# Stick-breaking attention in a decoder layer: query tiles 0 and 1, and 4 and 5, share one score slot in each pair step

## What is computed

```python
def block(args):                     # one query tile of 128 rows, all heads
    qi, i = args
    tpos = i * Q_BLOCK + jnp.arange(Q_BLOCK)
    z = jnp.einsum('bhqd,bhkd->bhqk', qi, k) * SCALE
    past = kpos[None, :] < tpos[:, None]
    log_fail = jnp.where(past, jax.nn.log_sigmoid(-z), 0.0)
    after = lax.cumsum(log_fail, axis=3, reverse=True) - log_fail
    a = jnp.where(past, jnp.exp(jax.nn.log_sigmoid(z) + after), 0.0)
    return jnp.einsum('bhqk,bhkd->bhqd', a, v)
```

## Time and profile before

| | us |
|---|---|
| median of three runs (1333.78 to 1333.85) | 1333.83 |
| the profiled execution's own time | 1333.74 |
| its span, from first to last instruction | 1331.9 |
| the eight pair steps, 119.6 to 606.4 | 486.8 |

### The profile page before, as it was taken

One profiled execution on the slowest core, in us unless ns is written; L12 is line 12 of the kernel. 1 busy time (PEld: TensorE's weight loads), 2 busy tenths in 40 slices (PEclk: granted clock), 3 DMA queues, 4 the chain that ended last, 5 costly groups with the idle time before them and its releaser, 6 DMA issues.

```text
span 1331.9 us, 20551 instructions
## 1 busy us (share of the span) xinstructions
PE 1316.9 (99%) x6854; PEld 1086.6 (82%) x6854; DVE 1032.5 (78%) x1185; ACT 684.3 (51%) x1202; POOL 418.1 (31%) x307
## 2 busy tenths in 40 slices
PE   7999999999999999999999999999999999999999
PEld 5887888888888888788888788888888888888887
DVE  7578989798888889995258877878778787777866
ACT  7577666667676667773244433343343434333340
POOL 2000000000000000213035754747556484654721
PEclk9999999999999999999999999999999999999999
DMA  7100110100010101205111222121212112121103
GB/s 253 32 25 25 32 33 17 32 24 24 24 38 17 31 25 40 96 25 166 48 40 32 71 72 63 42 72 31 71 47 63 56 39 71 39 71 60 43 32 127
DMA packets 91333, 71.50 MB, mean 54 GB/s; under 512 B 4240, under 2 KB 75920, under 8 KB 91280
## 3 DMA queue, kind: packets, MB, share of 16 engines
q1 hardware_dynamic: 91280, 70.81, 17.1%
HBM read 65.03 MB, written 4.19 MB: 52 GB/s over the span
## 4 chain that ended last, share of the span: by engine, by line
PE 92%; DVE 3%; ACT 2%; POOL 1%; issue 1%; DMA 0%; SPq 0%; ACTq 0%; POOLq 0%; DVEq 0%
PE ps L1419 27%; PE ps L346 17%; PE ps L1594 14%; PE ps L1125 7%; PE ps L402 5%; PE ps L386 5%; PE ps L376 4%; PE ps L1204 3%; PE ps L312 3%; PE ps L1649 2%; PE ps L901 1%; PE ps L841 1%; ACT junk L782 1%; PE ps L1012 1%; DVE a_l L598 1%
## 5 line engine op out<-in xcount | busy, mean ns | idle before, releaser
L1604 DVE TENSOR_TENSOR x<-ps,x 128x2048 f32<-128x2048 f32 x70 | 160.3, 2289 | 92.7 <-PE ps L1594 92.6
L605 POOL TENSOR_TENSOR o_t<-o_t,pv_low 128x256 f32 x24 | 22.9, 953 | 442.7 <-ACT o_t L490 442.7
L1387 DVE TENSOR_TENSOR part_l<-part_x,part_h 128x512 fp32r<-128x512 f32 x140 | 141.7, 1036 | 25.3 <-POOL part_x L1365 17.9
L1582 POOL TENSOR_TENSOR bl<-bx_B,bh 128x512 fp32r<-128x512 f32 x70 | 93.0, 1329 | 208.9 <-ACT bh L1578 208.9
L346 PE MATMUL ps<-hh,w_h 128*128 128x512 f32 x336 | 140.6, 418 | 0.0
L478 ACT ACTIVATE a_h<-ps 128x256 fp32r<-128x256 f32 (+2 forms) x96 | 78.0, 812 | 118.6 <-PE ps L386 118.0
L346 PE MATMUL ps<-hh,w_l 128*128 128x512 f32 x336 | 132.0, 393 | 0.0
L346 PE MATMUL ps<-hl,w_h 128*128 128x512 f32 x336 | 131.3, 391 | 0.0
L1419 PE MATMUL ps<-ft_h,part_h 128*128 128x512 f32 x320 | 124.5, 389 | 0.0
L1419 PE MATMUL ps<-ft_l,part_h 128*128 128x512 f32 x320 | 124.5, 389 | 0.0
L1419 PE MATMUL ps<-ft_h,part_l 128*128 128x512 f32 x320 | 124.5, 389 | 0.0
(11 more groups left out here) (288 smaller groups left out, 3392.7 us busy)
## 6 DMA issues: line engine op xcount, KB each, us to landing
w_raw<-in_sb_w_in SPq DMA_DIRECT2D x52, 256.0 KB, 2.9
bx_B<-in_w_down SPq DMA_DIRECT2D x44, 256.0 KB, 3.0
part_x<-in_w_gate SPq DMA_DIRECT2D x40, 256.0 KB, 2.9
part_x<-in_w_up SPq DMA_DIRECT2D x40, 256.0 KB, 2.9
wo_raw<-in_w_out SPq DMA_DIRECT2D x20, 256.0 KB, 2.9
x_in<-in_x SPq DMA_DIRECT2D x8, 512.0 KB, 7.7
x<-in_x SPq DMA_DIRECT2D x16, 256.0 KB, 6.2
out<-x SPq DMA_DIRECT2D x16, 256.0 KB, 2.0
```

What stands on the lines that cost most here:

```text
L1387: dve.tensor_tensor(part_l[m][p][:, :, :].rearrange(flat), part_x[m][p][:, :, :].rearrange(flat), part_h[p][:, :, :].rearrange(flat).bitca ...
L1582: pool.tensor_tensor(bl[(par + k) % 2][:, :], bx[B_OPS[k]][:, :], bh[(par + k) % 2][:, :].bitcast(F32), ALU.subtract).then_inc(s_bw, 1)
L1604: dve.tensor_tensor(o, ps[:, 0:4], o, ALU.add).then_inc(s_x2, 1)
```

## The change

`UNITS` gets ten entries. Tiles 0 and 1 become one slot (unit 0), the late chunks of tiles 4 and 5 another (unit 3); the slot numbers in `BOTH`. In such a slot tile i-1 lies in columns 0 to 127 and tile i in columns 144 to 399, so one ACT or DVE instruction on both is 400 columns a head. The other units move up. `pe_step` is unchanged in form, so scores of two slots are made at five places of a step. The values are still summed in six groups (`GROUPS`), at the units in `VALUES_AT`. For a shared slot both tiles stand in the upper 128 columns of `a_h`, and each matmul moves 128 columns. The projection of the next pair is dealt by `PARTS`. DVE scans the first head of unit 2 at u = 0 in every step, ahead of the weights and low parts there, and at u = 1 it does `dve_weights` before `dve_low`. The tables `CONV_AT`, `LOW_AT`, `PRE_AT`, `SPLIT_RATE`, `DVE_RATE`, `FILL` and `FILLED` are dealt anew for ten units; in step 6 a seventh head half is split ahead.

```diff
+    ODD_AT = P + 16
+    SPAN = ODD_AT + 2 * P
+    UNITS = [(1, 0, SPAN, True), (2, 0, 3 * P, True), (3, 0, BANK, True), (5, BANK, SPAN, True),
+             (4, 0, BANK, False), (5, 0, BANK, False), (6, BANK, 3 * P, True), (7, BANK, BANK, True),
+             (6, 0, BANK, False), (7, 0, BANK, False)]
+    BOTH = (0, 3)
...
+    GROUPS = [(0,), (1, 2), (3,), (4, 5), (6, 7), (8, 9)]
+    VALUES_AT = {1: 0, 2: 1, 3: 2, 5: 3, 7: 4, 9: 5}
+    ROWS_AT = {2: 0, 3: 2, 6: 5}
+    PARTS = {1: (0, 5, 8), 2: (1, 0, 8), 3: (2, 0, 8), 4: (3, 0, 4), 5: (3, 4, 8), 6: (4, 0, 4), 7: (4, 4, 8),
+             8: (5, 0, 4), 9: (5, 4, 8)}
+    EVAC_LOW = {2: 0, 3: 1, 4: 2, 6: 3}
-    LOW_AT = {0: 1, 2: 2, 3: 3, 6: 4, 7: 5, 10: 6}
+    LOW_AT = {0: 1, 1: 2, 3: 3, 4: 4, 5: 5, 8: 6}
+    def tiles_of(u):
+        i, _, w, _ = UNITS[u]
+        return ((i - 1, 0, P), (i, ODD_AT, 2 * P)) if u in BOTH else ((i, 0, w),)
 def pe_values
+            if u in BOTH:
+                parts = [(0, P, 0, 1, P), (P, 2 * P, 0, 2, P), (P, 2 * P, 1, 3, P)]
+            else:
+                w_first = UNITS[u - 1][2]
+                parts = [(0 if j * P < w_first else P, 2 * P, j, j, None) for j in range(w // P)]
             for h in range(2):
+                for b, (q0, q1, j, slot, col) in enumerate(parts):
                     for t, a in enumerate((a_h, a_l)):
+                        mm = pe.matmul(o_ps[:, h * 2 * P + q0:h * 2 * P + q1],
                                        v_s[par][:, k0 // P + j, 2 * h:2 * h + 2, :].rearrange("p a d -> p (a d)"),
+                                       a[:, h, slot, q0 if col is None else col:2 * P],
 def pe_step
                     pe_part(pe, s + 1, 1 - par, 0, 0, 2)
                     pe_transposes(pe, s, u)
-                    pe_part(pe, s + 1, 1 - par, 0, 2, 4)
+                    pe_part(pe, s + 1, 1 - par, 0, 2, 5)
                 elif not last:
-                    pe_part(pe, s + 1, 1 - par, u // 2, 4 * (u % 2), 4 * (u % 2) + 4)
+                    pe_part(pe, s + 1, 1 - par, *PARTS[u])
 def dve_scan
+                for _, at_, w in reversed(tiles_of(u)):
+                    back = f[:, at_:at_ + w + 1][:, ::-1]
+                    dve.tensor_tensor_scan(back, back, own[:, BANK - w:BANK + 1][:, ::-1], 0.0, ALU.mult, ALU.max
 def dve_step
-                if last and u == 0:
+                if u == 0:
                     dve_scan(dve, s, 2, 0)
-                if nxt and u and not (last and u == 1):
+                if nxt and u > 1:
                     dve_scan(dve, *nxt, 0)
...
+                if u == 1:
+                    dve_weights(dve, *nxt)
                 dve_low(dve, s, u)
-                if nxt and u:
+                if nxt and u > 1:
                     dve_weights(dve, *nxt)
...
+        PRE_AT = {2: EX[0:3], 3: EX[3:6], 5: EX[6:], 8: [("w", 0, 0), ("w", 1, 0)], 9: [("w", 2, 0), ("w", 3, 0)],
+        FILL = {0: [(0, (2, 3, 4, 5))], 1: [(1, (0, 1, 2, 3))], 2: [(1, (4, 5))], 3: [(2, None)], 4: [(3, LOWER)],
+                5: [(3, UPPER)], 6: [(4, None)], 7: [(5, None)], 8: [(6, None)], 9: [(7, None)]}
```

More of the change, by code:

```diff
@@ L50, in trunk, with blocks_of, group_of, home_of @@
     W0 = MW + 2
-    CONV_AT = {0: (2,), 2: (3,), 4: (4,), 5: (5,), 9: (6,), 11: (7,)}
-    LOW_AT = {0: 1, 2: 2, 3: 3, 6: 4, 7: 5, 10: 6}
+    CONV_AT = {0: (2,), 2: (3,), 3: (4,), 4: (5,), 7: (6,), 9: (7,)}
+    LOW_AT = {0: 1, 1: 2, 3: 3, 4: 4, 5: 5, 8: 6}
     GR = 4
-    assert NU % 2 == 0 and NU == 12
+    assert NU == 10
+    def tiles_of(u):
+        i, _, w, _ = UNITS[u]
+        return ((i - 1, 0, P), (i, ODD_AT, 2 * P)) if u in BOTH else ((i, 0, w),)
+    def blocks_of(u):
+        return [at_ + j * P for _, at_, w in tiles_of(u) for j in range(w // P)]
+    def group_of(u):
+        return [n for n, g in enumerate(GROUPS) if u in g][0]
+    def home_of(u):
+        n = len(blocks_of(u))
+        odd = u in BOTH or u == GROUPS[group_of(u)][1]
+        return slice(1 if u in BOTH else 0, n + (1 if u in BOTH else 0)), slice(P if odd else 0, 2 * P if odd else P)
     with ExitStack() as ctx:
@@ L168, in trunk @@
         x2 = [at(f"x2_{half}", [P, NT // 2, D], F32, a) for half, a in enumerate((ex_at, al_at))]
-        EX = [("o", k, 0) for k in range(6)]
+        EX = [("o", k, 0) for k in range(6)] + [("o", 0, 1)]
         ex_h = {i: at(f"ex_h{n}", [P, BANK], F32R, ex_at + n * 2 * KB) for n, i in enumerate(EX)}
@@ L341, in pe_part @@
                     pe.wait_ge(s_el, 4 * s + p)
-            if half == 0 and lo % 4 == 0:
-                pe.wait_ge(s_wl, W0 + 6 * s + 2 * b + lo // 4 + 1)
             for kc in range(lo, hi):
+                if half == 0 and kc % 4 == 0:
+                    pe.wait_ge(s_wl, W0 + 6 * s + 2 * b + kc // 4 + 1)
                 for i, (w, h) in enumerate(((wh, hh), (wh, hl), (wl, hh))):
@@ L372, in pe_scores @@
                 pe.wait_ge(s_fg, 2 * (NU * s + u - 2) + 2)
[L373 to L377, removed]
+            for i, at_, w in tiles_of(u):
+                for t, (q, kk) in enumerate(((q_h, k_h), (q_h, k_l), (q_l, k_h))):
+                    for h in range(2):
+                        r = slice(HD * h, HD * h + HD)
+                        mm = pe.matmul(z2[u % 2][:, h, at_:at_ + w], q[par][r, i * P:(i + 1) * P],
+                                       kk[par][r, k0:k0 + w], start=(t == 0), stop=(t == 2))
             mm.then_inc(s_z, 1)
         def pe_transposes(pe, s, u):
-            _, _, w, _ = UNITS[u]
             pe.wait_ge(s_a, NU * s + u + 1)
@@ L594, in dve_low @@
         def dve_low(dve, s, u):
[L595 to L596 removed]
+            js, cols = home_of(u)
             dve.wait_ge(s_th, 1 + TUSE * s + u + 1)
[L598 to L599 removed]
+            dve.tensor_tensor(a_l[:, :, js, cols],
+                              t_ps[:, :, 0:len(blocks_of(u)) * P].rearrange("p h (j q) -> p h j q", q=P),
+                              a_h[:, :, js, cols].bitcast(F32), ALU.subtract).then_inc(s_tl, 1)
         def pool_heads(pool, s, u):
@@ L624, in dve_step @@
                 nxt = (s, u + 1) if u + 1 < NU else (s + 1, 0) if not last else None
-                if last and u == 0:
+                if u == 0:
                     dve_scan(dve, s, 2, 0)
-                if nxt and u and not (last and u == 1):
+                if nxt and u > 1:
                     dve_scan(dve, *nxt, 0)
-                if u % 2 == 0 and 0 < u < 10 and not last:
-                    dve_evac_half(dve, s + 1, u // 2 - 1, 1 - par)
+                if u in EVAC_LOW and not last:
+                    dve_evac_half(dve, s + 1, EVAC_LOW[u], 1 - par)
                 if nxt and u:
```

103 lines of the change are left out of this document (45 added, 58 removed).

## The result

The changed kernel takes **1342.02 us** (1341.69 to 1342.06, 6 runs) against 1333.85 us before: a ratio of 1.0061, 95% interval 1.0048 to 1.0074. The forecast was 1342.0.

A forecast was written before the change was run, and what follows sets the result against it. TensorE was taken to bound the kernel, busy 1316.9 of 1331.9 us. Terms 7.0 - 3.2 + 3.75 + 2.0 - 1.3 = +8.25 us on 1333.74 gave 1342.0 us, own range 1339 to 1345, wider range 1336.5 to 1346.5.

The forecast's parts named there:

- Values, +7.0: Shared slots' values on PE: twelve 128-column matmuls paced by loads 0.11 us apart, 0.44 more a group, +7.0 us.
- rival 1: Shared values: short matmuls cheaper, 0.17 us a pair or 81 ns each, term 2.2, time 1337.2 us; chance 0.13.
- rival 4: Whole kernel faster: cheap shared values, first wait covered, later waits gone, -4.8 us, 1329 us; chance 0.07.
- Score place, -3.2: Five score places instead of six a step on PE, 0.40 us saved each, -3.2 us over eight steps.
- Wait at the beginning, +3.75: Steady step's beginning: PE waits for `w_l` and `a_l` behind DVE's scan, 0.75 us a step, +3.75 us for five.
- Rival 2: Step's beginning: the wait does not appear, ScalarE reaching `fail` earlier or PE's transposes slipping anyway; 1336 us; chance 0.07.
- Steady step: Steady pair steps in the loop: 61.4 us forecast instead of 60.2.
- Step 0, +2.0 of waits: First step: longer DVE chain up to `a_l` makes PE wait 3 us, about 1 already there; net +2.0 us.
- Steps 6 and 7, -1.3 of waits: Last two steps: waits of 1.25 us each instead of 1.9, -0.65 us each.
- Other slots, 0: Slots after unit 2: VectorE stays ahead of PE, tightest dates 0.25 us early at units 5 and 9; 0 us.
- rival 3: More waits: one 0.25 us reserve lost in each step, +0.5 us a step, 1346 us; chance 0.10.

The follow-up runs named there:

- Experiment 3: Kernel after with the shared slot's three value blocks stored side by side, eight value matmuls a group instead of twelve: 1335.50 us.
- experiment 6: Kernel before with the matmuls of both 256-column value groups cut into two of 128 columns: 1347.29 us.
- experiment 7: Kernel before with only one value group (tiles 0 and 1) cut into 128-column matmuls: 1342.70 us.
- Experiment 5: Kernel after with a sixth score place in every step but the last, between two halves of a projection: 1345.06 us.
- experiment 2: Kernel after with ScalarE's `fail` of unit 2 directly behind the copy of v, ahead of the four row copies: 1337.85 us.
- experiment 1: Kernel after with VectorE making `w_l` ahead of the scan of the 512-key tile at unit 0: 1338.55 us.
- Experiment 11: Kernel after with value blocks side by side, `fail` ahead of the low rows, and VectorE's low v ahead of two splits before the last step: 1330.19 us.
- experiment 4: Kernel after with value blocks side by side, plus `w_l` ahead of the scan: 1332.02 us; or plus `fail` ahead of the low rows: 1331.38 us.
- experiment 8: Kernel before with the tiles 0 and 1 value group cut, and 64 load-and-matmul pairs more at TensorE's program start: 1344.27 us.
- experiment 9: Kernel after with one more diagonal-unit value pair cut, 16 instructions more in TensorE's loop (1655 against 1639): 1350.80 us.
- experiment 10: Kernel after with value blocks side by side, `fail` ahead of low rows, `w_l` ahead of the scan, low v earlier in first and last steps: 1332.95 us.

## Why the prediction was right, point by point

- **Values, +7.0.** 1.29 us a group against 0.87: +0.42 for the 0.44 forecast, 16 x 0.42 = 6.7 us. Experiment 3 takes 6.5 back, experiments 6 and 7 bring 0.76 and 0.37 a step into the kernel before. Rivals 1 and 4, which needed a pair at 0.17 us, fall: the 0.06 between the first two starts is there once, at the head of the row, and the other eleven distances are 0.11 to 0.12. The rule of the Trainium skill, "TensorE: Matmul & The Clock Gate", section "LDWEIGHTS (loading the stationary operand)", gave 1.28 us for the twelve; the trace agrees with 1.29. The 81 ns that the Trainium skill's same page gives in its section "Back-to-back issue gap" do not hold for these rows, which are 108 ns apart on average (1.29 / 12).
- **Score place, -3.2.** Experiment 5 gives 0.42 a place for the 0.40 worked out from four distances: 8 x 0.42 = 3.4 us.
- **Wait at the beginning, +3.75.** `w_l` at 6.61 for 6.6, `a_l` at 7.48 for 7.5, the transposes at 7.53. Nine projections with the two halves of the wait take 2.90 us (311.84 to 314.74) where experiment 2's step leaves 2.22 and an undisturbed row 2.16: 0.68 to 0.74 a step, 3.4 to 3.7 us in all. The split between the halves was off: 0.53 was worked out for `w_l` and 0.22 for the transposes, measured are 0.67 and 0.06, since the matmul that waited also holds the next one for 0.10 more. Rival 2 falls, since `fail` did start at 3.74.
- **Steady step.** 0.84 + 0.74 - 0.42 = 1.16 against 1.11 measured and 0.48 + 0.75 = 1.23 forecast; 0.05 is left unexplained.
- **Step 0, +2.0 of waits.** The step is 2.64 longer; less 0.42 for values and place that is 2.2. The size was right and the place wrong: the chain was added up to `a_l`, but PE is held first at the transposes of unit 0, by `v_s` (1.0), which stands behind the scans of unit 1, and then by 0.3 for `w_l`. The 0.7 for `succ` was there before. A wait that comes first on the way hides part of the later one. Experiments 1 and 2 bear it out: both move `w_l`'s or the scan's date and leave step 0 at 64.20.
- **Ahead of step 0, 0.** It is +0.83, not forecast and not traced to a cause. The nine kernels of these runs that are built on the kernel after began step 0 between 119.8 and 120.5 us, the two built on the kernel before, without the shift, at 119.7 and 120.1, so half of it may be the execution's own.
- **Steps 6 and 7, -1.3 of waits.** The stretch from step 6 to the end is 0.86 shorter, less twice 0.42 that is 1.7 us of waits gone. Those for `succ` and most for `a_l` are; in their place `v_s` in step 7, 0.2 before, has become 1.0, because the transposes of unit 0 now come when VectorE still writes the two splits ahead of it. Experiment 11 turns that order round and gets 1.2 us back.
- **Other slots, 0.** No wait of PE is recorded in slots 2 to 9 of the steady steps; rival 3 falls. The reserve was real: with the step 1.4 us shorter, in experiment 4, there is still none.

By stage the forecast was 5 x 1.23 = 6.15 for the steady steps, 2.0 + 0.48 = 2.5 for step 0 and 2 x 0.48 - 1.3 = -0.3 for the rest; measured are 5.54, 2.64 and -0.86, and 0.83 ahead of step 0. So the steady steps and the end were forecast 1.1 us too high together, and the unforecast 0.83 and step 0 made 1.0 of it good. That the forecast total is closer than its terms is luck; without the 0.83 the time would have been 1341.2.

The instruction fetch of experiments 6 to 9 has no part in the 8.2 us: behind the loop's first iteration the kernels before and after fetch nothing. It was a risk that the prediction did not name: by the medians it cost 5.6 to 7.4 us in the three kernels that it struck.

## What to carry to other kernels

Fewer and wider instructions on engines with time to spare buy nothing by themselves; read what their layout and their dates do to the bounding engine. Here two free-standing prices, matmuls cut so short that their weight loads, 0.11 us apart, set the pace, and one scan that sits ahead of two operands, cost nearly four times the gain of 0.42 us a step, and both were taken off again, one by a layout and one by an order. When an instruction is moved up a queue, its operand's date has to move with it, as experiments 2 and 10 show from both sides.

## What the runs showed of the hardware

- A change between 64-row and 128-row matmuls costs PE about 0.1 us ahead of it and 0.1 behind it, so 0.42 us for a score place in the middle of projections, although no wait is recorded.
- Instructions come in packets of 16 KB, and a change of TensorE's loop alone can make them come in every iteration. It goes with the body's length and with where it lies: bodies of 1619 (the kernel before) and 1639 instructions (after) ran without a fetch behind the first iteration; 1635 and 1651, which start where the 1619 does, stalled 2.3 to 2.6 us at the turns; the 1635 ran clean when it lay 128 instructions later; and 1655 stalled 2.3 us where 1639 had not. The stall shows as "issue", with the q8 instruction queue active inside the loop, and a lower granted clock can follow it (0.95 and 0.97 over the step). Which alignment or size decides was not found, nor why one kernel stalled at one turn only.
- In experiment 10 waits of PE of 0.6, 1.0 and 1.0 us in step 0 were followed by a granted clock of 0.57 (132 to 134 us of the profiled execution); the mean clock shows a fall in eight of the eleven executions and none in three. The waits of 0.7, 1.0 and 0.3 us in the same step of the kernel after were not followed by one (1.00 over the step).
